# Stick-breaking attention on TensorE: the two heads of a pair issued piece by piece in turn, the logits two turns ahead

## The reference, cut to what matters

```python
def _stick_breaking_block(qb, kb, vb, start):
    z = jnp.einsum('bhqd,bhkd->bhqk', qb, kb)
    visible = jnp.arange(nk)[None, :] < (start + jnp.arange(nq))[:, None]
    log_keep = jnp.where(visible, jax.nn.log_sigmoid(-z), 0.0)
    later = lax.cumsum(log_keep, axis=3, reverse=True) - log_keep
    w = jnp.where(visible, jnp.exp(jax.nn.log_sigmoid(z) + later), 0.0)
    return jnp.einsum('bhqk,bhkd->bhqd', w, vb)
```

## Time and profile before

| | |
|---|---|
| median of three runs | 1533.17 us |
| the profiled execution's own time | 1533.31 us |
| its span (first to last instruction) | 1531.5 us |
| TensorE busy | 1397.3 us, 91% |
| VectorE, ScalarE, GpSimd busy | 723.8, 530.5, 597.6 us |
| chain of waits that ended last | TensorE 77%, VectorE 14%, ScalarE 5% |
| mean granted clock of TensorE | 0.942 of 2.4 GHz |
| L873, L898, L924, L896 in that chain | 2%, 2%, 1%, 2% of the span |

### The profile page before, as it was taken

The page is one execution under the profiler, slowest core; times in us unless marked ns, Lnnn a source line. Parts: engine busy times, 40 slices in busy tenths (PEclk is TensorE's granted clock), DMA queues, the critical chain, the costliest instruction groups (busy, mean ns, idle before and its releaser), DMA issues.

```text
span 1531.5 us, 19840 instructions
## 1 busy us (share of the span) xinstructions
PE 1397.3 (91%) x8564; PEld 1225.5 (80%) x8564; DVE 723.8 (47%) x993; ACT 530.5 (35%) x726; POOL 597.6 (39%) x224
## 2 busy tenths in 40 slices
PE   6977559998799999999988999999879999999996
PEld 5977545568699999999977998898757888888874
DVE  7994992334754201431434555756366420144044
ACT  3253414762432212321235433434434221223122
POOL 2424512313643443343554312314455434343450
PEclk8989766999899999999989999999989999999997
DMA  5311000001122332333321111221122333333321
GB/s 165 108 56 56 0 1 1 0 27 57 55 83 84 103 91 83 99 95 83 88 78 56 56 58 52 63 71 55 63 80 63 102 94 99 90 103 97 96 56 55
DMA packets 142038, 108.13 MB, mean 71 GB/s; under 512 B 8096, under 2 KB 139376, under 8 KB 141952
## 3 DMA queue, kind: packets, MB, share of 16 engines
q1 hardware_dynamic: 141552, 106.77, 23.4%
q10 hardware_dynamic: 400, 0.11, 0.0%
HBM read 104.77 MB, written 2.10 MB: 70 GB/s over the span
## 4 chain that ended last, share of the span: by engine, by line
PE 77%; DVE 14%; ACT 5%; issue 2%; POOL 2%; DMA 0%; DVEq 0%; SPq 0%; POOLq 0%; ACTq 0%
PE pb L631 60%; PE pb L689 2%; DVE uqk L1658 2%; PE pb L690 2%; PE pb L691 2%; DVE h L1839 2%; PE pb L873 2%; PE pb L898 2%; PE pb L1003 1%; PE pb L699 1%; PE pb L924 1%; DVE h L1825 1%; PE pb L896 1%; ACT tmp L1165 1%; DVE h L1810 1%
## 5 line engine op out<-in xcount | busy, mean ns | idle before, releaser
L494 POOL TENSOR_TENSOR wl<-raw,wh 128x2048 fp32r<-128x2048 f32 x97 | 454.0, 4681 | 676.8 <-ACT wh L1099 676.8
L631 PE MATMUL pb<-hh,wh 128*128 128x264 f32 (+1 forms) x1376 | 362.3, 322 | 30.0 <-ACT hh L1332 19.5
L631 PE MATMUL pb<-hh,wl 128*128 128x264 f32 (+1 forms) x1376 | 355.5, 317 | 0.0
L631 PE MATMUL pb<-hl,wh 128*128 128x264 f32 (+1 forms) x1376 | 349.4, 315 | 0.6 <-POOL hl L526 0.6
L631 PEld LDWEIGHTS pb<-hh,wh 128*128 128x128 f32 x1376 | 231.4, 193 | 52.5 <-issue 25.9
L631 PEld LDWEIGHTS pb<-hh,wl 128*128 128x128 f32 x1376 | 230.5, 192 | 15.6
L631 PEld LDWEIGHTS pb<-hl,wh 128*128 128x128 f32 x1376 | 227.8, 191 | 17.5 <-POOL hl L526 1.5
L631 PE MATMUL pb<-hidh,wh 128*128 128x264 f32 (+1 forms) x768 | 205.6, 321 | 3.5 <-POOL wl L494 3.5
L631 PE MATMUL pb<-hidh,wl 128*128 128x264 f32 (+1 forms) x768 | 203.9, 319 | 0.0
L631 PE MATMUL pb<-hidl,wh 128*128 128x264 f32 (+1 forms) x768 | 203.1, 318 | 0.0
L1099 ACT ACTIVATE wh<-raw 128x2048 fp32r<-128x2048 f32 x97 | 184.9, 1907 | 1.5 <-DMA raw<-in_w_in_c 1.4
(11 more groups left out here) (359 smaller groups left out, 1841.6 us busy)
## 6 DMA issues: line engine op xcount, KB each, us to landing
raw<-in_mlp_w_up SPq DMA_DIRECT2D x32, 1024.0 KB, 5.4
raw<-in_mlp_w_down SPq DMA_DIRECT2D x32, 1024.0 KB, 5.5
raw<-in_w_in_c SPq DMA_DIRECT2D x16, 1024.0 KB, 5.4
raw<-in_w_in_ab SPq DMA_DIRECT2D x8, 1024.0 KB, 5.9
raw<-in_w_out_ab SPq DMA_DIRECT2D x4, 1024.0 KB, 5.0
raw<-in_w_out_c SPq DMA_DIRECT2D x4, 1024.0 KB, 4.9
x_tok<-in_x SPq DMA_DIRECT2D x2, 1024.0 KB, 7.7
out_h<-o_tok SPq DMA_DIRECT2D x4, 512.0 KB, 3.1
```

The source lines that it names most:

```text
L494: pool.tensor_tensor(wl[:, c % RING, :], raw[:, c % RING, :], wh[:, c % RING, :].bitcast(F32), ALU.subtract).then_inc(w_lo, 1)
L631: mm = pe.matmul(pb[:, bank + b, 0:z_ - a], lhs, rhs[:, a:z_], start=first and hi and k == 0, stop=last and k == len(todo) - 1)
```

## The change

It reorders TensorE's work of the attention stage and takes a couple of units (two heads, one kind) as its step j. The logits of the two heads are issued piece by piece in turn (head 0, head 1, head 0, ...), the 400 and 512 columns of kinds 1 and 2 as two pieces each; then both masks. The value products of the two heads are issued in turn as well, kinds 1 and 2 in one piece for each head. A turn of the loop is the sums of both units, the value products of the couple before, and the logits of the couple after the next. ScalarE's order stays; the weights have four buffers instead of three, and the wait for them counts couples.

```diff
-        w_att = sb("w_att", [P, 3, 512], F32, m0b)
+        w_att = sb("w_att", [P, 4, 512], F32, m0b)
...
+            def z_pair(j):
+                i, s = divmod(j, 3)
+                if j == 2:
+                    pe.wait_ge(s5_y, 4 + FREE)
+                if j >= 3:
+                    pe.wait_ge(w_ready, 2 * j - 4)
+                parts = [[(0, 16, L - P, 512), (16, 160, 384, 384), (160, 432, 256, 256)],
+                         [(0, 200, 128, 128), (200, 400, 128, 328)],
+                         [(0, 256, 0, NMETA), (256, 512, 0, NMETA + 256)]][s]
+                for first, (c0, c1, k0, q0) in enumerate(parts):
+                    for hd, ps in enumerate(halves_of):
+                        pe.matmul(pb[:, 2 * s + hd, c0:c1], uqk[ps, i + 8, k0:k0 + P], uqk[ps, i + 4, q0:q0 + c1 - c0],
+                                  start=first == 0, stop=False, skip_group_check=True)
+                c, mask = [(288, hide_r[:, 0:288]), (P, hide_r[:, 16:144]), (P - NMETA, hide_r[:, 32:144])][s]
+                for hd in range(2):
+                    pe.matmul(pb[:, 2 * s + hd, 0:c], ident_r[:, :], mask, start=False, stop=False,
+                              skip_group_check=True).then_inc(z_ready, 1)
...
+            def pv_pair(j):
+                i, s = divmod(j, 3)
+                pe.wait_ge(w_ready, 2 * j + 2)
+                if j == 0:
+                    pe.wait_ge(w0_ready, 1)
+                elif s == 0:
+                    pe.wait_ge(o_evac, i)
+                parts = [[(496, 4, 0, 16), (368, 3, 16, 160), (240, 2, 160, 432)], [(112, 1, 0, 400)], [(0, 0, 0, 512)]][s]
+                for n, (c0, b, w0_, w1) in enumerate(parts):
+                    for hd, ps in enumerate(halves_of):
+                        h8 = 2 * i + hd
+                        mm = pe.matmul(pb[ps, 6 + i % 2, c0:512], v0[:, b, 64 * h8:64 * h8 + 64],
+                                       w_att[:, (2 * j + hd) % 4, w0_:w1], start=s == 0 and n == 0, stop=s == 2,
+                                       skip_group_check=True)
+                mm.then_inc(pv_done, 2)
...
             z0()
-            z(0)
-            z(1)
+            z_pair(0)
             acc0()
-            for g in range(NUNIT):
-                acc(g)
-                ...
+            z_pair(1)
+            for j in range(NUNIT // 2):
+                acc(2 * j)
+                acc(2 * j + 1)
+                if j == 0:
+                    pv0()
+                else:
+                    pv_pair(j - 1)
+                if j + 2 < NUNIT // 2:
+                    z_pair(j + 2)
+            pv_pair(NUNIT // 2 - 1)
...
-                if g >= 3:
-                    act.wait_ge(pv_done, g - 2)
-                act.activation(w_att[:, g % 3, 0:c], pb[:, n, 0:c], ACT.Exp).then_inc(w_ready, 1)
+                if g >= 4:
+                    act.wait_ge(pv_done, g - 2 - g % 2)
+                act.activation(w_att[:, g % 4, 0:c], pb[:, n, 0:c], ACT.Exp).then_inc(w_ready, 1)
```

More of the change, by code:

```diff
@@ L911, in acc @@
                 mm.then_inc(acc_ready, 1)
[L913 to L918, removed]
+            def pv_pair(j):
+                i, s = divmod(j, 3)
+                pe.wait_ge(w_ready, 2 * j + 2)
+                if j == 0:
                     pe.wait_ge(w0_ready, 1)
-                elif n == 0:
+                elif s == 0:
                     pe.wait_ge(o_evac, i)
[L923 to L933, removed]
-                else:
-                    mm = part(0, 0, w[:, 0:512], stop=True)
-                mm.then_inc(pv_done, 1)
@@ L938, in _ @@
-            z0()
-            z(0)
-            z(1)
-            acc0()
-            for g in range(NUNIT):
-                acc(g)
[L944 to L953, removed]
+                parts = [[(496, 4, 0, 16), (368, 3, 16, 160), (240, 2, 160, 432)], [(112, 1, 0, 400)], [(0, 0, 0, 512)]][s]
@@ new lines, in pv_pair @@
+                for n, (c0, b, w0_, w1) in enumerate(parts):
[5 more added lines that the diff above has]
+                mm.then_inc(pv_done, 2)
+            z0()
+            z_pair(0)
@@ L956, in _ @@
+            acc0()
+            z_pair(1)
[4 more added lines that the diff above has]
+                    pv0()
+                else:
+                    pv_pair(j - 1)
+                if j + 2 < NUNIT // 2:
+                    z_pair(j + 2)
+            pv_pair(NUNIT // 2 - 1)
             run("glu", hh, hl, lambda n: (y_ready, n + 1), cols_=512, kcs=4)
```

## The result

The changed kernel takes 1507.12 us (median of four runs, 1506.67 to 1508.98), the kernel before beside it 1533.98; the ratio is 0.9828, 95% interval 0.9814 to 0.9843, some 27 us less. The forecast was 1514.7 with 1509.0 to 1523.0: right in its sign, 8 us short in its size, and the range missed the time by 2 us. The profiled execution took 1506.95 us with a span of 1504.9, TensorE busy for 1366.1 of them (91%) at a mean granted clock of 0.947.

The account below looks back on a forecast made before the run. TensorE, busy in nearly all of the attention stage, was taken to bound it; savings of 9.4 (first stretch), 8.8 (two periods) and 0.4 (last), together 18.6, from 1533.31 gave 1514.7 us, range 1509.0 to 1523.0.

Parts of the forecast that it names:

- What bounds the stage, and that overlap decides: Attention stage: TensorE is busy in nearly all of it, so the gain depends on whether interleaved half-array calls overlap.
- the weak witness: L859, the only evidence for overlap by columns: 16 records in 0.97 us at half clock, read as two side by side.
- The slots: Interleaved two-record calls: B1 runs beside A2, B2 beside the next A1, so seven calls make 8 slots.
- the rival to which I gave 0.12: A pair costs one call: one slot less per group, 1.6 us a period, half lost to ScalarE's chain; 1512, chance 0.12.
- The sums: Second sum of each couple no longer follows a value product: 3 x 0.14 to 0.19, 0.5 us saved per pair of heads.
- both periods: Stretch 270.37 to 314.79 us, two pairs of heads: 17.8 us each instead of 22.2, 8.8 us less.
- The clock: Stage start: granted clock rises at 249 us instead of 256.3; 246 to 260 not excluded, a us later costs 0.47.
- stretch (c): First sums to end of first pair's value products, 229.03 to 270.37 us: 31.9 us instead of 41.3, 9.4 less.
- The waits: TensorE waits on the softplus of each pair's sixth unit: 0.8 us a period, 2.4 us in the last.
- The tail's own forecast of 0.4: Last stretch of the stage, 13.92 us: only 0.4 us saved, since TensorE waits 2.4 us there.
- Fourth buffer and two turns ahead: Fourth weight buffer and logits issued two turns ahead: no gain or cost, since their waits are already covered.
- the slow rival: Clock stays at 1.2 GHz through the stage: slower, 1561 us, chance 0.04.

Follow-up runs that it names:

- logits only: Kernel before with only the two heads' logits interleaved and split, one couple ahead, old sums, value products and buffers: 1518.75 us, ratio 0.9897.
- values apart: Changed kernel with the two heads' value products apart (sums, values of head 0, sums, values of head 1): 1513.01 us, ratio 0.9859.
- extra products: Extra matrix products into an unused bank ahead of the stage: kernel before 1534.69 us, changed kernel 1504.69, changed with the S5 gate moved earlier 1499.86.
- masks between: Changed kernel with each head's mask directly behind its logits, so the logits can't overlap: 1525.66 us, ratio 0.9941.
- second logits apart: Changed kernel with only the second couple's logits, the first inside the stage, head by head with the mask between: 1512.51 us, ratio 0.9847.
- sequence of four: Changed kernel with all of head 0's pieces before head 1's, kinds 1 and 2 in four pieces each: 1515.48 us, ratio 0.9875.
- gate early: Changed kernel with ScalarE's three S5 gate activations moved behind the first couple's exponential, ahead of the copy of the outputs: 1499.77 us, ratio 0.978.
- the second experiment: Changed kernel with all pieces of head 0 before those of head 1, in logits and value products: 1507.6 us, ratio 0.9824.

## Why the prediction was right or wrong

- **What bounds the stage, and that overlap decides**: right. Both halves, by rows (logits only) and by columns (values apart), overlap fully; the weak witness told the truth.
- **The slots**: wrong, and with it "A call A is records A1, A2, ...; B1 is issued behind A2 and runs beside it". B1 runs beside A1. A couple costs what one head's calls cost: 0.87, 1.05 and 1.13 us for logits (forecast 1.03, 1.27, 1.34 with the fixed part), 0.82, 1.00 and 0.97 for values (1.15, 1.43, 1.18). That is the rival to which I gave 0.12, a pair for the cost of one. The Trainium skill (TensorE: Matmul & The Clock Gate, Part 3) has matmuls on different parts of the array cost hardly more together than one alone, and the trace agrees on the cost. In a period the slots were 1.5 us too dear: logits with masks saved 3.5 us instead of 2.94, value products 2.8 instead of 1.80. The sums gave 0.05 instead of 0.5 back (9.16 us before, 9.11 after, counted from start to start without the waits), so that term had no worth. TensorE's work in a period fell to 15.90 us instead of 16.9, but the period only to 17.03 instead of 17.8: with less work of its own TensorE waits more for the gate's chain. The rival's "half of it lost to ScalarE's chain" was about right: 1.5 us for both periods.
- **The clock**: wrong, and the larger term. I took the rise from the first stretch in which sums and value products followed without logits, 249 us, and wrote that no row excludes 246 to 260; it came at 236.7. The premise was a wrong reading of the trace of before. The stretch from 249.87 was not the first such one: 236.89 to 245.21 is another, 8.3 us long, and the clock stayed low through all of it (the last row has the columns of the earlier trace rows):

```profile
236.62 0.47 PE L886 MATMUL pb<-hide_r,ident_r 128*128 128x128 f32 x1
236.89 1.75 PE L898 MATMUL pb<-sp,ntri 128*128 128x432 f32 x2
...
245.21 2.07 PE L873 MATMUL pb<-uqk 64*128 64x512 f32 x2
...
236.89:245.21 8.32, 8.32 (x37) 5.47 (x37) 2.05 (x6) 2.58 (x6) 0.00 (x0) 0.50 0.00 0
```

Compared with the half clock of 20.0 us in the sum, 6.7 us at a factor 1.9 is 13.3 x 0.47 = 6.3 us of the 7.5 that stretch (c) beat its forecast by. The experiments show the cause as far as an edit can: where the second couple's logits overlap fully, the rise is 6.6 to 7.5 us in all seven profiled kernels that enter with a low clock and no extra products; where they don't (masks between, second logits apart) or do in part (sequence of four), 17.3 to 20.5 us. Each is one profile, and one unprofiled run of second apart was as fast as an early rise would make it. The order of the sums, to which I had tied it, is not needed for the early rise: the old order with overlapped logits rises at 7.4. Without that overlap the new order rose earlier than the old (20.5 us with masks between, for 27.2 and 24.3), so it may have a part there, which no run separates. What in the overlap raises the clock stays open.
- **The waits**: right in place and size (0.91 for 0.8 and 2.27 for 2.4), and the experiment with the gate early shows their cause. A third, 0.21 us a period, was not forecast. The tail's own forecast of 0.4 saved became 0.5 lost, since the clock fell behind the 2.27 us wait. It did so in five profiled kernels with a wait of 2.17 or 2.27 us there, but not in second apart (2.27) or the sequence of four (2.08), so these 1.6 us are partly chance.
- **The sum of the misses**: clock 6.3, the rest of (c) 1.2, periods 1.5, tail -0.9, together 8.1 us, the distance between 81.0 and 72.8.
- **Fourth buffer and two turns ahead**: costed at nothing, and no wait on them appears. Neither was undone by itself, so what the longer lead brings is not shown; from logits only (0.46 us wait, period 19.39) to values apart (18.73, no wait in the steady part) it is at most 0.7 us a period, if the two orders cost the same otherwise.
- **The range** took the rise of the clock from 246 on and so ended 2 us too high. A clock that had behaved oddly before (27 busy us at half speed) was a reason to widen it downwards as well as to keep the slow rival.

How much of the 27 us is clock? In the traces the time at half clock in the stage fell from 27.2 us to 6.7 at the start and 3.5 in the tail, 17 us at 0.47: about 8 us. The other 19 are work that runs side by side, less TensorE's new waits. This split is worked out, not measured by an edit that moves the clock alone.

## What to carry to other kernels

If two groups of matmuls use different halves of the array, put them next to each other, with no full-array call between: each couple then costs one group, whether interleaved or, for up to four records a group, simply one behind the other; splitting pieces further brought nothing here. When TensorE gets shorter, walk the in-order queue that feeds it before counting the gain: here moving three activations into a place where ScalarE waited anyway gave 7 us on top (6.0 of it in the stage), about as much as the missed clock. Where the granted clock is low in a stage, treat its rise as a range of its own, in both directions, and look for every stretch that fits the supposed cause, above all those after which it did not rise.

## What the runs showed of the hardware that I had not expected

- A matmul record on one half of the array's rows starts together with the record on the other half that stands four ahead of it in program order, past the three between; with six or eight records in front of it, it started no earlier than that (1.37 us for 1.13, and 1.64 for 1.05). The Trainium skill (TensorE: Matmul & The Clock Gate, Part 3) says that matmuls keep program order in start and end; between the two halves the trace of the second experiment shows otherwise, and the measurement decides.
- TensorE can be busy for 17 to 27 us on end and stay at 1.2 GHz, and one couple of half-array calls side by side instead of one behind the other can end this 10 us earlier. Outside the stage, in the trace of before, the longest that TensorE is busy at half clock without a break is 6.1 us, and the dense projection behind the stage has the clock back after 5.
- The remainder of the span, behind the start of the next projection and untouched by any edit, took 1198.4 us in the profile of the gate-early kernel, 1202.8 before, 1202.1 changed and 1204.4 with the extra products before. The part ahead of the stage varies too: the first sums start between 229.0 and 233.0 us, and the changed kernel (229.98) and logits only (232.96) have the same order of work up to there. So 3 or 4 us either way of a total may come from a part that nobody changed, and the stage in the trace is the sharper measure. Why these parts differ is not shown.
